# Sigmoid by tanh in a two-block transformer kernel, with its small transfers and one modulation chunk moved

## The reference

```python
cond = jax.nn.silu(c)                        # each block: conditions of the modulation
mod = cond @ ada_w[i] + ada_b[i]

a, g = jnp.split(h @ w_in + b_in, 2, axis=-1)        # block 1, layer 0: convolution
u = a * jax.nn.sigmoid(g)
u = depthwise_conv_31_taps(u) + dw_b
u = jax.nn.silu(layer_norm(u, ln_g, ln_b))
y = u @ w_out + b_out

out = (o * jax.nn.silu(z)) @ w_out                   # block 2, layer 1: windowed attention
```

## Time and profile before

| | |
|---|---|
| three runs | 1271.3, 1271.72, 1275.79 us; median 1271.72 |
| profiled execution | 1271.3 us, of which the span of the trace is 1269.5 |
| TensorE busy | 1198.7 us (94%) |
| VectorE, ScalarE, GpSimd busy | 875.2 (69%), 546.7 (43%), 48.9 us (4%) |
| stream | 210 loads of 1 MB; 233.6 MB in all, mean 184 GB/s |

### The profile page before, as it was taken

One profiled execution on the slowest core, in us unless ns is written; L12 is line 12 of the kernel. 1 busy time (PEld: TensorE's weight loads), 2 busy tenths in 40 slices (PEclk: granted clock), 3 DMA queues, 4 the chain that ended last, 5 costly groups with the idle time before them and its releaser, 6 DMA issues.

```text
span 1269.5 us, 20700 instructions
## 1 busy us (share of the span) xinstructions
PE 1198.7 (94%) x8804; PEld 1092.1 (86%) x8804; DVE 875.2 (69%) x1304; ACT 546.7 (43%) x712; POOL 48.9 (4%) x69
## 2 busy tenths in 40 slices
PE   2898989999999979999999999999999999998996
PEld 1886889999999858999999999888888888887676
DVE  6766876677777665688877675676756773676644
ACT  2423466455354375664455412332212221555763
POOL 0000000000000021000000000000000000000640
PEclk9899989999999989999999999999999999999899
DMA  9697447787848621676765353333443342231000
GB/s 386 227 336 260 181 179 287 292 315 267 299 177 322 241 104 67 228 259 243 256 242 187 146 189 143 113 122 131 138 162 133 133 161 97 100 133 68 1 2 34
DMA packets 37788, 233.64 MB, mean 184 GB/s; under 512 B 4656, under 2 KB 9008, under 8 KB 10432
## 3 DMA queue, kind: packets, MB, share of 16 engines
q1 hardware_dynamic: 35136, 229.99, 49.0%
q10 hardware_dynamic: 2560, 2.33, 0.8%
HBM read 226.60 MB, written 1.05 MB: 179 GB/s over the span
## 4 chain that ended last, share of the span: by engine, by line
PE 83%; DVE 7%; ACT 5%; issue 3%; DMA 2%; POOL 0%; SPq 0%; ACTq 0%; DVEq 0%
PE prod L1468 24%; PE prod L1470 24%; PE prod L1469 24%; DMA raw<-stream 2%; ACT w_hi L534 2%; PE misc L1406 2%; PE misc L1456 2%; DVE w_lo L884 1%; PE misc L1580 1%; DVE raw L917 1%; PE prod L1665 1%; PE misc L1429 1%; PE prod L1437 1%; PE misc L1677 1%; PE prod L1456 1%
## 5 line engine op out<-in xcount | busy, mean ns | idle before, releaser
L884 DVE TENSOR_TENSOR w_lo<-raw,w_hi 128x2048 fp32r<-128x2048 f32 x135 | 309.2, 2291 | 279.9 <-ACT w_hi L534 279.7
L534 ACT ACTIVATE w_hi<-raw 128x2048 fp32r<-128x2048 f32 x135 | 258.4, 1914 | 489.3 <-PE prod L1470 466.2
L1468 PE MATMUL prod<-XH,w_hi 128*128 128x256 f32 (+1 forms) x1312 | 407.1, 310 | 6.9 <-DVE w_lo L884 3.8
L1469 PE MATMUL prod<-XL,w_hi 128*128 128x256 f32 (+1 forms) x1312 | 400.9, 306 | 0.0
L1470 PE MATMUL prod<-XH,w_lo 128*128 128x256 f32 (+1 forms) x1312 | 400.6, 305 | 0.0
L1468 PEld LDWEIGHTS prod<-XH,w_hi 128*128 128x128 f32 x1312 | 251.4, 192 | 23.3 <-DVE w_lo L884 4.5
L1469 PEld LDWEIGHTS prod<-XL,w_hi 128*128 128x128 f32 x1312 | 251.4, 192 | 11.4 <-issue 0.7
L1470 PEld LDWEIGHTS prod<-XH,w_lo 128*128 128x128 f32 x1312 | 251.4, 192 | 10.6
L1468 PE MATMUL prod<-FH,w_hi 128*128 128x256 f32 (+1 forms) x640 | 195.1, 305 | 0.0
L1470 PE MATMUL prod<-FH,w_lo 128*128 128x256 f32 (+1 forms) x640 | 194.7, 304 | 0.0
L1469 PE MATMUL prod<-FL,w_hi 128*128 128x256 f32 (+1 forms) x640 | 194.7, 304 | 0.0
(11 more groups left out here) (239 smaller groups left out, 1292.0 us busy)
## 6 DMA issues: line engine op xcount, KB each, us to landing
raw<-stream SPq DMA_DIRECT2D x210, 1024.0 KB, 4.8
FH<-V SPq DMA_DIRECT2D x16, 71.0 KB, 3.5
FH<-V ACTq DMA_DIRECT2D x16, 71.0 KB, 3.5
FL<-V SPq DMA_DIRECT2D x16, 71.0 KB, 4.2
FL<-V ACTq DMA_DIRECT2D x16, 71.0 KB, 4.0
X<-x_features SPq DMA_DIRECT2D x1, 1024.0 KB, 10.5
V<-cond_rows SPq DMA_DIRECT2D x1, 1024.0 KB, 6.9
C<-ctx_features SPq DMA_DIRECT2D x1, 1024.0 KB, 6.8
```

The lines of the kernel that those rows point to most:

```text
L534: A(halves(w)[0].rearrange("p k c -> p (k c)"), raw[:, n % RING, :], ACT.Copy).then_inc(weight_hi, 1)
L884: ins = tt(lo.rearrange("p k c -> p (k c)"), raw[:, n % RING, :], hi.rearrange("p k c -> p (k c)").bitcast(F32), ALU.subtract)
L1468: mm(out, lhs_hi, rhs_hi, start=start, stop=False)
L1469: mm(out, lhs_hi, rhs_lo, start=False, stop=False)
```

## The change

Every Sigmoid on ScalarE becomes a Tanh of half the argument, and VectorE turns it into the sigmoid with one tensor_scalar, `0.5 * t + 0.5`, in place, followed by a wait for its own result: one of 128x1024 at the start, four of 128x512 in the gates of the convolution, eight of 128x256 in the layer norm's SiLU, one of 128x2048 for `cond_2` (in pass 64, a pass ahead of the multiply), and four of 128x512 in `b_z`. The biases of these functions are halved at the start: ScalarE fills `half_b` with three copies of 128x8 where one filled `beta_x`. The output stays the same function of the inputs.

Three more things move. The transfers of `WS` and `BS` (512 KB each) and of three small tables (192, 64 and 64 KB), issued behind the loads of units 16, 20 and 24, are issued together behind that of unit 8. The transfer of `cond_2` (1 MB) moves from behind unit 32's load to behind unit 44's. In `MOD_BEFORE` one chunk is placed ahead of unit 44 and the one ahead of unit 53 goes; the order of the chunks among themselves stays, so eight of them come a place earlier.

```diff
-    46, 47, 48, 49, 50, 51, 52, 53,
+    44, 46, 47, 48, 49, 50, 51, 52,
...
-        beta_x = sb("beta_x", [P, KT])
+        half_b = sb("half_b", [P, 24])
...
-                if n == WHERE[MLP0 + 20]:
+                if n == WHERE[QKV]:
                     sp.wait_ge(acts_lo, SET[2])
                     sp.dma_start(cond_2, cond_in[:, 1:3, :]).then_inc(cond_loaded, 16)
...
-                if n == WHERE[MLP0 + 4]:
+                if n == WHERE[CONV_OUT]:
                     sp.dma_start(WS[:, :, :], ws_in).then_inc(params_loaded, 16)
-                if n == WHERE[MLP0 + 8]:
                     sp.dma_start(BS[:, :, :], bs_in).then_inc(params_loaded, 16)
-                if n == WHERE[MLP0 + 12]:
                     for dst, name in ((alibi, "alibi"), (by_head, "by_head"), (spread, "spread")):
...
-                        A(EV[:, j % 2, i * T:(i + 1) * T], tiles(w, T)[:, i, :], ACT.Sigmoid,
-                          bias=cl("conv_b_in", 8 + 2 * j + i)).then_inc(gate_sigmoid, 1)
+                        A(EV[:, j % 2, i * T:(i + 1) * T], tiles(w, T)[:, i, :], ACT.Tanh,
+                          bias=half_b[:, 2 * j + i:2 * j + i + 1], scale=0.5).then_inc(gate_tanh, 1)
...
-                    A(EV[:, j % 2, :].rearrange("p (i t) -> p i t", i=2), tiles(w, T), ACT.Sigmoid)\
-                        .then_inc(z_sigmoid, 1)
+                    A(EV[:, j % 2, :].rearrange("p (i t) -> p i t", i=2), tiles(w, T), ACT.Tanh, scale=0.5)\
+                        .then_inc(z_tanh, 1)
...
-                            A(TS[:, k, :], H[:, k, :], ACT.Sigmoid, bias=cl("conv_ln_b", k))\
-                                .then_inc(silu_sigmoid, 1)
+                            A(TS[:, k, :], H[:, k, :], ACT.Tanh, bias=half_b[:, 8 + k:9 + k], scale=0.5)\
+                                .then_inc(silu_tanh, 1)
                         if k >= 2:
-                            act.wait_ge(silu_done, k - 1)
+                            act.wait_ge(silu_step, 2 * (k - 2) + 2)
...
-            A(beta_x[:, :], cl("ln_b_2", 0, 8), ACT.Copy, scale=ALPHA).then_inc(beta_ready, 1)
-            act.wait_ge(beta_ready, 1)
+            A(half_b[:, 0:8], cl("conv_b_in", 8, 8), ACT.Copy, scale=0.5).then_inc(half_ready, 1)
+            A(half_b[:, 8:16], cl("conv_ln_b", 0, 8), ACT.Copy, scale=0.5).then_inc(half_ready, 1)
+            A(half_b[:, 16:24], cl("ln_b_2", 0, 8), ACT.Copy, scale=ALPHA).then_inc(half_ready, 1)
+            act.wait_ge(half_ready, 3)
...
+            def sigmoid_cond(part, t):
+
+                dve.wait_ge(cond_tanh, part)
+                ts(t, t, 0.5, 0.5, ALU.mult, ALU.add).then_inc(cond_ready, 1)
+                dve.wait_ge(cond_ready, 2 * part - 1)
+
...
-                    dve.wait_ge(gate_sigmoid, 2 * (j + 1))
+                    dve.wait_ge(gate_tanh, 2 * (j + 1))
+                    ts(g, g, 0.5, 0.5, ALU.mult, ALU.add).then_inc(gate_half, 1)
+                    dve.wait_ge(gate_half, j + 1)
...
-                    dve.wait_ge(z_sigmoid, j + 1)
+                    dve.wait_ge(z_tanh, j + 1)
+                    ts(e, e, 0.5, 0.5, ALU.mult, ALU.add).then_inc(z_half, 1)
+                    dve.wait_ge(z_half, j + 1)
...
-                            dve.wait_ge(silu_sigmoid, i + 1)
+                            dve.wait_ge(silu_tanh, i + 1)
+                            ts(TS[:, i, :], TS[:, i, :], 0.5, 0.5, ALU.mult, ALU.add)\
+                                .then_inc(silu_step, 1)
+                            dve.wait_ge(silu_step, 2 * i + 1)
...
+                if s == COND_2_UNIT - 2:
+                    sigmoid_cond(2, cond_t)
```

More of the change, by code:

```diff
@@ L370, in build @@
         cond_loaded = sem("cond_loaded")
-        cond_sigmoid = sem("cond_sigmoid")
+        cond_tanh = sem("cond_tanh")
         cond_ready = sem("cond_ready")
         gqk_ready = sem("gqk_ready")
-        beta_ready = sem("beta_ready")
+        half_ready = sem("half_ready")
         dot_done = sem("dot_done")
@@ L396, in build @@
         padded = sem("padded")
-        gate_sigmoid = sem("gate_sigmoid")
-        silu_sigmoid = sem("silu_sigmoid")
-        silu_done = sem("silu_done")
+        gate_tanh = sem("gate_tanh")
+        gate_half = sem("gate_half")
+        silu_tanh = sem("silu_tanh")
+        silu_step = sem("silu_step")
         y_ready = sem("y_ready")
@@ L434, in build @@
         g_lo = sem("g_lo")
-        z_sigmoid = sem("z_sigmoid")
+        z_tanh = sem("z_tanh")
+        z_half = sem("z_half")
         sink_negated = sem("sink_negated")
@@ L780, in _ @@
             act.wait_ge(cond_loaded, 16)
-            A(cond_t[:, 0, :], cond[:, 0, :], ACT.Sigmoid).then_inc(cond_sigmoid, 1)
+            A(cond_t[:, 0, :], cond[:, 0, :], ACT.Tanh, scale=0.5).then_inc(cond_tanh, 1)
             act.wait_ge(params_loaded, 32)
-            A(beta_x[:, :], cl("ln_b_2", 0, 8), ACT.Copy, scale=ALPHA).then_inc(beta_ready, 1)
-            act.wait_ge(beta_ready, 1)
+            A(half_b[:, 0:8], cl("conv_b_in", 8, 8), ACT.Copy, scale=0.5).then_inc(half_ready, 1)
+            A(half_b[:, 8:16], cl("conv_ln_b", 0, 8), ACT.Copy, scale=0.5).then_inc(half_ready, 1)
+            A(half_b[:, 16:24], cl("ln_b_2", 0, 8), ACT.Copy, scale=ALPHA).then_inc(half_ready, 1)
+            act.wait_ge(half_ready, 3)
             act.wait_ge(x_loaded, 16)
@@ L808, in _ @@
                     act.wait_ge(cond_loaded, 32)
-                    A(cond_t, cond_2, ACT.Sigmoid).then_inc(cond_sigmoid, 1)
+                    A(cond_t, cond_2, ACT.Tanh, scale=0.5).then_inc(cond_tanh, 1)
                 if s == MIX_B + 2:
@@ L816, in _ @@
                         act.wait_ge(x_restored, k + 1)
-                        A(X[:, k, :], X[:, k, :], ACT.Identity, bias=beta_x[:, k:k + 1],
+                        A(X[:, k, :], X[:, k, :], ACT.Identity, bias=half_b[:, 16 + k:17 + k],
                           scale=ALPHA).then_inc(x_scaled, 1)
@@ L891, in split_lo @@
                     ins.then_inc(unit_consumed, 2 if w + 1 in AHEAD else 1)
+            def sigmoid_cond(part, t):
+                dve.wait_ge(cond_tanh, part)
+                ts(t, t, 0.5, 0.5, ALU.mult, ALU.add).then_inc(cond_ready, 1)
+                dve.wait_ge(cond_ready, 2 * part - 1)
             def silu_cond(part, dst, c, t):
-                dve.wait_ge(cond_sigmoid, part)
                 tt(dst, t, c, ALU.mult).then_inc(cond_ready, 1)
-                dve.wait_ge(cond_ready, part)
+                dve.wait_ge(cond_ready, 2 * part)
             def dots(n, pieces=(0, 1)):
@@ L1311, in boundary @@
                             i = k - 1
-                            dve.wait_ge(silu_sigmoid, i + 1)
+                            dve.wait_ge(silu_tanh, i + 1)
+                            ts(TS[:, i, :], TS[:, i, :], 0.5, 0.5, ALU.mult, ALU.add)\
+                                .then_inc(silu_step, 1)
+                            dve.wait_ge(silu_step, 2 * i + 1)
                             stt(out=TS[:, i, :], in0=H[:, i, :], scalar=cl("conv_ln_b", i),
-                                in1=TS[:, i, :], op0=ALU.add, op1=ALU.mult).then_inc(silu_done, 1)
+                                in1=TS[:, i, :], op0=ALU.add, op1=ALU.mult).then_inc(silu_step, 1)
                         if k >= 3:
@@ L1331, in _ @@
             dve.wait_ge(padded, 1)
+            sigmoid_cond(1, cond_t[:, 0, :])
             silu_cond(1, cond[:, 0, :], cond[:, 0, :], cond_t[:, 0, :])
```

## The result

| | before | after |
|---|---|---|
| median of 7 runs each, us | 1275.79 (1271.3 to 1278.95) | 1281.73 (1278.94 to 1283.95) |
| profiled execution; its span | 1271.3; 1269.5 | 1279.83; 1278.0 |
| ratio of the times | | 1.0058, 95% interval 1.0038 to 1.0078 |

The change makes the kernel slower by 0.58%: 7.4 us by the ratio (4.8 to 10.0), 8.5 by the two profiled executions, 5.9 between the two medians shown. The forecast was +7.5 us and 1278.8, with a range of its own of 1276.5 to 1281.5; the median measured, 1281.73, lies above that range. The added time was about right, but it was added to a time before that was too low: in four series with 7, 31, 21 and 22 runs the median of the kernel before was 1275.79, 1273.01, 1273.72 and 1273.01, not 1271.72.

A forecast was written before the change was run, and what follows sets the result against it. TensorE was taken to bound the kernel, with 83% of the chain that ended last. Terms 0.45 + 2.56 + 2.85 + 1.2 + 0.45 = 7.5 us, added to the profiled 1271.3, gave 1278.8; range 1276.5 to 1281.5.

The forecast's parts named there:

- fourth convolution: Before the last convolution: the fourth gate's tensor_scalar delays L1048 and the shift transfers TensorE waits for, +0.45 us.
- SiLU, eight tiles: Ahead of `conv_out`: VectorE has no gap, so eight more operations and waits cost 8 x 0.32 = +2.56 us (1.7 to 3.5).
- the DMA stall behind it: Behind the SiLU: dot products free the load slots, so the later stall moves too and absorbs nothing, 0.
- QKV: load, chunk, order: Between units 43 and 44: `w45` lands at 353.9, the new chunk's dot products follow, sums end at 365.3: +2.85 us.
- QKV: clock: TensorE stands some 2.9 us behind unit 43; a lower clock may then cost 0 to 2.35 us, half taken: 1.2.
- first `b_z`: The first tensor_scalar stands ahead of L1119, and TensorE waits for L1134 behind it: +0.45 us.
- part 5: `WS`, `BS` and tables moved near 76 us: shift copies up to 3.4 later, cost 0, up to +2 if SP's queue fills.
- QKV stays covered: Rival, chance 0.22: `w45` lands by 351.4, QKV costs 0.2 us and no clock; 3.7 us in all, 1275.0.
- full clock: Rival, chance 0.20: the load at QKV is late but TensorE keeps full clock; 6.3 us in all, 1277.6.
- adds nothing: Rival, chance 0.04: nothing added on the path, 1271.3, only if ScalarE and not VectorE paces the SiLU part.
- faster: Rival, chance 0.02: attention 2 waited for the table load at 1170.84 and added VectorE work is hidden; 1270.0.
- Conv stage clogged: Rival, chance 0.10: SP held near 76 to 85, third convolution waits some 2 us on top of the 7.5; 1280.8.

The follow-up runs named there:

- the filled kernel: Changed kernel plus six idle matmuls ahead of the last sums before QKV and five ahead of the rotary product behind the second `b_z`: 1281.82 us, ratio 1.0055.
- The moves alone: Kernel before with only the moved transfers and chunks, its functions still Sigmoid: 1278.19 us, ratio 1.0036.
- the functions alone: Changed kernel with the moved transfers and chunks taken back, leaving Tanh and the tensor_scalars: 1277.03 us, ratio 1.0035.
- the doubled operation: Changed kernel with a second tensor_scalar (times 1, plus 0) and its wait on each of the eight SiLU tiles: 1287.3 us, ratio 1.0102.

## Why the prediction was right and wrong

Term by term, the offsets of the profiled execution against the terms of the sum:

| place | term | measured |
|---|---|---|
| fourth convolution | 0.45 | 0.93 |
| SiLU, eight tiles | 2.56 | 2.63 |
| the DMA stall behind it | 0 | -0.86 |
| QKV: load, chunk, order | 2.85 | 3.0 |
| QKV: clock | 1.2 | 1.9 |
| first `b_z` | 0.45 | 2.04 |
| behind it | 0 | -1.17 |
| in between | 0 | 0.07 |
| sum | 7.5 | 8.5 |

At QKV the offsets give only the 4.90 together. The 1.9 is what the rows show of the clock, and the 3.0 is what is left.

- **The base.** The step that failed is the one from the sum to the time: "The profiled execution took 1271.3 (span 1269.5), 0.4 below the median shown, 1271.72. Forecast: 1271.3 + 7.5 = 1278.8, 0.56% above the median." The profiled execution lies not 0.4 but 1.7 to 4.5 us below the median of longer series. A change of 7.5 on 1273.0 to 1275.8 is 1280.5 to 1283.3, and 1281.73 was measured. Three runs with a spread of 4.5 us could not carry a base known to 0.4. The size of the change came out well (7.4 by the ratio) partly by luck: the terms were off by +0.5, +0.7 and +1.6 and by -0.9 and -1.2, which leaves only 1.0 in the sum.
- **SiLU: right,** 0.32 forecast for an operation and 0.33 measured, by none, one and two of them.
- **The stall behind it** absorbed some: 6.89 before, 6.03 after. That the stall "moves too and absorbs nothing" was wrong by 0.86 in this execution. From unit 10 to unit 13 five other kernels with the same layer norm and the same chunks there went from 1.07 us made good to 0.92 lost, so one execution does not size this term, and why it varies wasn't tried.
- **The gates and the other transfers:** the fourth convolution was 0.93 late, but 0.68 of it is there at unit 0, ahead of any gate, where the fourteen profiled kernels differ by 1.0 us among themselves. So the 0.45 can neither be confirmed nor refuted. "So 0" of part 5 was wrong for the third convolution: the shift copies landed 3.2 us later, as its bound of 3.4 had it, and TensorE waited 0.61 us for them, which is one of the signs named for "wrong". Most of it was gone at the fourth, which waited 1.25 instead of 1.70.
- **QKV, the load: right.** `w45` forecast to land at 353.9, plus the 2.7 us by which the kernel was behind: 356.6; its copy began at 356.68. The sums were forecast to end at 365.3 + 2.7 = 368.0 at full clock; they ended at 369.19, and 1.0 of the 1.2 between is the clock. The two causes were shown apart, 2.1 and 2.25 us of the wait, by taking back either.
- **QKV, the clock:** taken at half, 1.2; it came nearly whole: 1.0 on the sums (16 in 2.69 us; at the rate of before, 24 in 2.57, they would take 1.71) and 0.95 on the four keep_busy records (1.92 against 0.97). This term and `b_z` are the two of the sum that were mis-sized most.
- **`b_z`:** +0.45 for the tensor_scalar was right (TensorE waited 2.58 us for L1145 instead of 2.12, and the filled kernel lost 0.44). What was not costed is the clock behind it: the wait before was 2.12 us at full clock, and 0.46 more of it was followed by a clock of 0.74 and another 1.6 us. The moves alone, which leave this place as it was, lost nothing here. But one kernel lost the 1.6 us behind a wait of 2.11 and one kept its clock behind 2.58, so whether this execution paid them was in part chance.
- **The table load** of attention 2 went, 17 loads instead of 18: Exp starts at 1181.90 with no load ahead of it, released by VectorE after 1.67 us of idle time; before, the load of 1.28 and 0.37 of waiting stood in the same gap. It is worth 0, by the rows. The Trainium skill ("ScalarE: Activation LUTs", Table sets) lists tanh in the set of exp, and the trace agrees; the 2.7 us that the page gives for a switch are not seen here.
- **The condition vectors** were free, as forecast: the first tensor_scalar ran from 5.55 to 6.24, and VectorE still waited 1.73 us for the first `raw` load behind it; the large one ran at 547.70, with 0.72 us of waiting left.
- **The rivals:** "QKV stays covered" fell with the wait of 4.51 us; "full clock" with the 0.50; "adds nothing" and "faster" with the period of 1.45. "Conv stage clogged" came in small, 0.61 us at the third convolution, and in full only with two entries more in the stream, when the fourth waited 10.30 us.

Of the 1.17 us made good behind `b_z`, 0.28 come before unit 135 in every kernel with Tanh in `b_z`. The other 0.89, in attention 2, go with the clock. In both kernels TensorE has a stretch at half clock there; in the changed kernel it lies earlier against the work. Of the 4 us from 1170 in the kernel before (1179.41 in the changed one, the same work by the offset of unit 135) the granted clock is 0.80 before and 0.56 after, with TensorE busy for 1.8 and 2.4 us only; eight us later, with TensorE busy throughout, it is 0.50 and 0.66, then 0.92 and 1.00. Three other kernels with this pattern made good 0.8 to 0.9 us there; those with the functions alone, with the Sigmoid kept in the layer norm and with the doubled operation have the pattern of the kernel before and did not. What stays open: what decides where these stretches fall, and why shift issues took 0.8 us longer in one execution.

## What to carry to other kernels

An operation costs what it takes only where its engine has no gap; the same 0.3 to 0.45 us was free where VectorE had a gap, full price in the layer norm, and at the first `b_z` 0.46 us in one profiled execution and about 2 in eight, by the clock behind it. So cost a longer TensorE wait not by its length alone but also with a chance for a lower granted clock behind it, look in the profile of before for waits of TensorE behind which the clock still stood at 1.00, and do not take one profiled execution for the rule: the same wait went either way here. And where transfers are issued in program order, a moved transfer is weighed against what is queued behind it: one megabyte ahead of a critical load cost 2.2 us, while the same kind of move elsewhere cost 0.6 us at one wait and nothing in the total that could be measured, until two more entries came in front. A base for a forecast of half a per cent wants more than three runs.

## What the hardware showed beyond that

- TensorE's clock: in the four kernels in which TensorE stood still for 2.39 to 10.30 us ahead of the fourth convolution, its 128 matmuls took 8.41 to 9.94 us; in the eight where it stood for 0.99 to 2.22, they took 7.11. At the first `b_z` the same lengths gave no such order: 2.58 us was followed by a clock of 1.00 in one kernel, and 2.11 by a fall to 0.50 in another.
- Idle matmuls hold the clock only where they stand. In the doubled kernel they kept it at 1.00 from 112 to 128, and it went to 0.50 from 144 to 152, where TensorE waited for VectorE's tiles. Put ahead of QKV in the kernel before with two chunks moved, whose TensorE had no gap of that kind there, six of them kept the clock at 1.00 and the place still cost 2.1 us instead of 0.65.
- A tensor_scalar of 128x256 took 0.29 us and of 128x512 0.42; each with a wait on its own result costs 0.33 and 0.46 from start to start.
